# Sample value products with the probabilities standing, and the combination of three groups batched over tiles

## What is computed

```python
# latent attention of a sample token: rows = 1024 cached rows of its batch and the new one
p = mla_probs(q, k_nope, kr, inv, mask)
ctx = einsum('bhqt,btr->bqhr', p, rows[..., :KV_LORA])      # value product, 8 heads, 128 features
o_mla = einsum('bqhr,rhd->bqhd', ctx, w_uv)
# dilated attention of a sample token, for each of three groups: 128, 128 and 64 cached rows are valid
o = einsum('bhqj,bqjhe->bqhe', p, vg)                       # value product, 4 heads of 128 features
# combination of the three groups, for prompt and sample tokens
wts = softmax(stack(lses), axis=0)
o = einsum('gbsh,gbshe->bshe', wts, stack(outs))
```

## Time and profile before

| what | us |
|---|---|
| median of 3 runs (4493.37 to 4502.63) | 4498.88 |
| span of the profiled execution | 4461.3 |
| PE busy in it | 3866.2 |
| DVE busy | 2746.1 |
| ACT busy | 1193.5 |
| sample stage of latent attention | 446 to 622 |
| combination and dilated sample stage | 1411 to 1539 |

### The profile page before, as it was taken

One profiled execution on the slowest core, in us unless ns is written; L12 is line 12 of the kernel. 1 busy time (PEld: TensorE's weight loads), 2 busy tenths in 40 slices (PEclk: granted clock), 3 DMA queues, 4 the chain that ended last, 5 costly groups with the idle time before them and its releaser, 6 DMA issues.

```text
span 4461.3 us, 43547 instructions
## 1 busy us (share of the span) xinstructions
PE 3866.2 (87%) x14598; PEld 2550.7 (57%) x14598; DVE 2746.1 (62%) x6469; ACT 1193.5 (27%) x3201; POOL 861.8 (19%) x717
## 2 busy tenths in 40 slices
PE   7789879999995699977999677879999999899986
PEld 5458357798984588865444344434444445454443
DVE  1665535352345311236999997766779766976876
ACT  2356333232222101122222367621111111111111
POOL 0000000100000000001333323333333333343332
PEclk8889869997697599988999889999999999999997
DMA  4000200312114311125888879999999999999997
GB/s 152 5 2 1 55 38 22 117 45 85 60 48 152 105 43 43 62 92 194 310 316 328 326 306 354 384 418 414 413 398 379 414 412 410 373 394 414 389 357 286
DMA packets 252635, 1016.82 MB, mean 228 GB/s; under 512 B 25434, under 2 KB 100594, under 8 KB 167426
## 3 DMA queue, kind: packets, MB, share of 16 engines
q0 software_dynamic: 101520, 723.10, 40.9%
q1 hardware_dynamic: 130722, 280.49, 17.1%
q10 hardware_dynamic: 20176, 10.49, 0.8%
HBM read 964.74 MB, written 49.25 MB: 227 GB/s over the span
## 4 chain that ended last, share of the span: by engine, by line
PE 26%; DVE 15%; DMA 11%; issue 2%; ACT 2%; POOL 0%; SPq 0%; ACTq 0%; DVEq 0%
PE banks L2357 9%; PE banks L2343 8%; DMA ff_room<-in_v 8%; DVE ff_rows L2006 4%; PE banks L2332 4%; PE banks L2280 2%; DVE ff_acc L1972 2%; DMA gates_dram<-ff_room 1%; PE banks L2225 1%; DMA ff_rows<-in_uv,pk_expert 1%; DVE pk_eq L1662 1%; DVE pk_axes L1667 1%; DVE mx_x L2032 1%; PE banks L2304 1%; DVE pk_besti L1641 1%
## 5 line engine op out<-in xcount | busy, mean ns | idle before, releaser
L1904 POOL DMA_INDIRECT ff_rows<-in_uv,pk_expert x640 | 806.0, 1259 | 1507.6 <-DVE ff_acc L1972 828.4
L2006 DVE CUSTOM_DVE_ANT_0 ff_rows<-ff_rows,ff_h_row 128x1024 f32<-128x1024 f32 x648 | 766.4, 1220 | 43.9 <-DMA ff_rows<-in_uv,pk_expert 42.0
L2357 PE MATMUL banks<-ff_room,mx_x 128*128 128x512 f32 x1536 | 703.1, 609 | 59.0 <-DVE mx_x L2047 32.5
L2343 PE MATMUL banks<-mx_x,ff_room 128*128 128x384 f32 x2048 | 683.4, 487 | 10.9 <-ACT mx_x L2190 10.4
L2343 PEld LDWEIGHTS banks<-mx_x,ff_room 128*128 128x128 f32 x2048 | 389.3, 190 | 310.3 <-issue 73.5
L2332 PE MATMUL banks<-ff_rows,o_mla_tops 128*128 128x512 f32 x904 | 445.5, 642 | 138.3 <-ACT o_mla_tops L2100 134.7
L2357 PEld LDWEIGHTS banks<-ff_room,mx_x 128*128 128x128 f32 x1536 | 297.6, 195 | 420.6 <-issue 359.0
L1972 DVE SCALAR_TENSOR_TENSOR ff_acc<-ff_rows,ff_a,ff_acc 128x1024 f32<-128x1024 f32 x388 | 498.6, 1285 | 7.2
L2332 PEld LDWEIGHTS banks<-ff_rows,o_mla_tops 128*128 128x128 f32 x904 | 178.7, 206 | 355.4 <-issue 198.0
L176 PE MATMUL banks<-d_w_high,h_high 128*128 128x512 f32 (+1 forms) x648 | 275.7, 425 | 30.7 <-DVE d_w_low L183 29.8
L2088 ACT ACTIVATE ff_gelu<-ff_dots 128x2 f32<-128x2 f32 x324 | 65.7, 203 | 822.8 <-DVE ff_dots L2006 822.5
(11 more groups left out here) (379 smaller groups left out, 5942.9 us busy)
## 6 DMA issues: line engine op xcount, KB each, us to landing
ff_room<-in_uT SPq DMA_DIRECT2D x128, 512.0 KB
ff_room<-in_v SPq DMA_DIRECT2D x128, 512.0 KB
gates_dram<-ff_room SPq DMA_DIRECT2D x6, 4096.0 KB, 16.6
mx_x<-gates_dram SPq DMA_DIRECT2D x128, 192.0 KB
d_w<-in_w_dil POOLq DMA_DIRECT2D x9, 2048.0 KB, 12.7
d_w<-in_w_ada POOLq DMA_DIRECT2D x32, 512.0 KB, 4.7
ff_room<-in_w_pq SPq DMA_DIRECT2D x32, 512.0 KB
ff_rows<-in_uv,pk_expert POOLq DMA_INDIRECT x640
```

The costliest lines, as they stand in the source:

```text
L1904: pool.indirect_dma_start(out=rows[r][:, :], out_offset=None, in_=IN["uv"][:, :], in_offset=bass.IndirectOffsetOnAxis(ap=at, axis=0))\
L2006: ins = dve.tensor_tensor_reduce(rows[r][:, 0:D], rows[r][:, 0:D], h_row[i % 2][:], 1.0, 0.0, ALU.mult, ALU.add, dots[:, B % RB, j:j + 1])
L2343: ins = pe.matmul(SD[:, 0:ND], u[e % 4][:, k, :], hd[:, k, :], start=(k == 0), stop=(k == KD - 1))
L2357: ins = pe.matmul(Y[j][:, half], ad[e % 2][:, j * P:(j + 1) * P], v[e % 4][:, half_rows[half]], start=(e == 0), stop=(e == NK - 1))
```

## The change

- Latent attention: pT has 32 columns for each page and batch, 8 of them with probabilities and 24 zero (DVE zeroes the whole at the stage's start). The value product takes these 32 columns as the standing operand and the 128 columns of values as the moving one; batch 4i + k writes partitions 32k of bank i. ACT copies each bank's 128 columns to cr, and two products with picked columns of the identity turn them back and place them beside the new token's product, which now comes behind.
- Dilated sample: the same with 512 columns of values moving, for 3 groups and 8 batches; the third group holds two batches on the two halves of the partitions, and zeros in pT leave out the other one. ACT copies the first bank of results, DVE the second, and for each head two products with picked columns turn them back.
- The loads of the third group's pairs are cut in four, two for each half of the partitions.
- Combination: the statistics of all tiles are loaded once, by three DMAs of ACT's queue, in pieces of 32 bytes; the weights are made once for all tiles. The first product of each tile moves to ACT (semaphore first), in front of the copies of the values in ACT's list, and y has two buffers. ACT copies a turned tile one tile later. SP issues pairs 0 and 1 ahead of x(0), and each tile's pairs ahead of its x. DVE does a tile's keys ahead of its mixing.

```diff
+        pT = sb("pT", [P, NPAGE, NSA, M])
...
+                pe.wait_ge(s["zero"], 1)
+                for i in range(2):
+                    for j in range(NPAGE):
+                        for k in range(4):
+                            b = 4 * i + k
+                            ins = pe.matmul(c.ps[i][k * M:(k + 1) * M, 0:KVL], pT[:, j, b, :], rows[:, b * NPAGE + j, 0:KVL],
+                                            start=(j == 0), stop=(j == NPAGE - 1))
+                    ins.then_inc(s["ctx"], 1)
                 pe.matmul(c.ps[3][:, 0:R], c.lat_s[:, 0:KVL], pTn[:], start=True, stop=False)
-                for b in range(NSA):
-                    for j in range(NPAGE):
-                        last = b == NSA - 1 and j == NPAGE - 1
-                        ins = pe.matmul(c.ps[3][:, b:R:NSA], rows[:, b * NPAGE + j, 0:KVL], pT[:, j, b:R:NSA],
-                                        start=False, stop=last)
-                ins.then_inc(s["ctx"], 1)
+                of_batch = c.ps[3][:, 0:R].rearrange("p (h b) -> p h b", b=NSA)
+                picked = c.ident[:].rearrange("p (k h) -> p h k", h=M)[:, 0:MH]
+                for i in range(2):
+                    pe.wait_ge(s["ctxr"], i + 1)
+                    ins = pe.matmul(of_batch[:, :, 4 * i:4 * i + 4], cr[:, i], picked, start=False, stop=(i == 1))
+                ins.then_inc(s["ctxt"], 1)
...
+                act.wait_ge(s["zero"], 1)
+                act.activation(pT[:, :, :, 0:MH].rearrange("p j b h -> p j h b"),
+                               c.ps[4][:].rearrange("p (j h b) -> p j h b", h=MH, b=NSA), ACT.Copy).then_inc(s["ptc"], 1)
                 act.activation(pTn[:], c.ps[5][0:NSA, 0:R], ACT.Copy).then_inc(s["ptc"], 1)
+                for i in range(2):
+                    act.wait_ge(s["ctx"], i + 1)
+                    act.activation(cr[:, i], c.ps[i][:, 0:KVL], ACT.Copy).then_inc(s["ctxr"], 1)
...
+                dve.memset(pT[:], 0.0).then_inc(s["zero"], 1)
...
+        x = [sb(f"x{i}", [P, NG, GW]) for i in range(2)]
+        stats = sb("row_stats", [P, NG, NT, 2 * DH])
...
+        pT = sb("pT", [P, NG, NSA, M])
...
                 for t in range(NT):
-                    if t >= 2:
-                        sp.wait_ge(s["y"], t - 1)
-                    sp.dma_start(x[t % 2][:], c.dram["o_group"][:, t * P:(t + 1) * P, :]
-                                 .rearrange("g p w -> p g w")).then_inc(x_in[t % 2], 16)
                     for i in after[t]:
...
+                        if g < 2:
+                            sp.dma_start(kv[i % NB][:], state.rearrange("b p f -> p b f")).then_inc(kv_in[i % NB], 16)
...
+                        else:
+                            for k in range(2):
+                                at = slice(k * n, (k + 1) * n)
+                                sp.dma_start(kv[i % NB][at, 0], state[k]).then_inc(kv_in[i % NB], 16)
+                                sp.dma_start(qb[i % NB][at, 0], q[k * GW:(k + 1) * GW].unsqueeze(0).to_broadcast([n, GW]))\
+                                    .then_inc(kv_in[i % NB], 16)
+                    if t >= 2:
+                        sp.wait_ge(s["y"], t - 1)
+                    sp.dma_start(x[t % 2][:], c.dram["o_group"][:, t * P:(t + 1) * P, 0:GW]
+                                 .rearrange("g p w -> p g w")).then_inc(x_in[t % 2], 16)
...
+                def weights():
+                    nm, sm = stats[:, :, :, 0:DH], stats[:, :, :, DH:]
+                    dve.wait_ge(s["stats"], 16 * NG)
...
+                    dve.wait_ge(s["first"], t + 1)
+                    for g in range(1, NG):
                         for h in range(DH):
                             cols = slice(h * DE, (h + 1) * DE)
-                            if g == 0:
-                                ins = dve.tensor_scalar(Y[:, cols], X[:, g, cols], e[:, g, h:h + 1], None, ALU.mult)
-                            else:
-                                ins = dve.scalar_tensor_tensor(out=Y[:, cols], in0=X[:, g, cols],
-                                                               scalar=e[:, g, h:h + 1], in1=Y[:, cols],
-                                                               op0=ALU.mult, op1=ALU.add)
+                            ins = dve.scalar_tensor_tensor(out=y[t % 2][:, cols], in0=x[t % 2][:, g, cols],
+                                                           scalar=e[:, g, t, h:h + 1], in1=y[t % 2][:, cols],
+                                                           op0=ALU.mult, op1=ALU.add)
...
-                    weights(t)
+                    for n, i in enumerate(after[t]):
+                        keys(i)
+                        if t == 0 and n == 0:
+                            weights()
                     mix(t)
-                    for i in after[t]:
-                        keys(i)
...
+                dve.wait_ge(s["pv"], 2)
+                dve.tensor_copy(ors[:, 1], O[1][:]).then_inc(s["o_rows"], 1)
...
             def _(act):
-                for t in range(NT):
-                    act.wait_ge(s["diff"], t + 1)
-                    act.activation(e[:], e[:], ACT.Exp).then_inc(s["exp"], 1)
-                    for i in after[t]:
-                        g, b = pairs[i]
-                        n = KROWS[g]
-                        act.wait_ge(kv_in[i % NB], 32 * (i // NB + 1))
-                        act.activation(V[g][0:n, b:b + 2, :], kv[i % NB][0:n, :, GW:], ACT.Copy).then_inc(s["vv"], 1)
+                for g in range(NG):
+                    act.dma_start(stats[:, g], c.dram["o_group"][g, :, GW:].rearrange("(t p) w -> p t w", p=P))\
+                       .then_inc(s["stats"], 16)
+                act.dma_start(diag[:], IN["diag"][0:R]).then_inc(s["mask"], 16)
+
+                def turned(t):
                     act.wait_ge(s["turn"], t + 1)
                     act.activation(c.o_dilT[:, :, t * P:(t + 1) * P],
                                    c.ps[t % 2][:].rearrange("p (k q) -> p k q", q=P), ACT.Copy).then_inc(s["copy"], 1)
+
+                for t in range(NT):
+                    if t == 0:
+                        act.wait_ge(s["diff"], 1)
+                        act.activation(e[:], e[:], ACT.Exp).then_inc(s["exp"], 1)
+                        act.wait_ge(s["diff"], 2)
+                    act.wait_ge(x_in[t % 2], 16 * (t // 2 + 1))
+                    if t >= 2:
+                        act.wait_ge(s["turn"], t - 1)
+                    for h in range(DH):
+                        cols = slice(h * DE, (h + 1) * DE)
+                        ins = act.activation(y[t % 2][:, cols], x[t % 2][:, 0, cols], ACT.Copy, scale=e[:, 0, t, h:h + 1])
+                    ins.then_inc(s["first"], 1)
+                    for i in after[t]:
+                        act.wait_ge(kv_in[i % NB], landed(i))
+                        dst, src = values(i)
+                        act.activation(dst, src, ACT.Copy).then_inc(s["vv"], 1)
+                    if t:
+                        turned(t - 1)
+                turned(NT - 1)
...
+                act.wait_ge(s["zero"], 2)
                 act.wait_ge(s["pt"], 1)
-                act.activation(pT[:], N2[:, 0:NG * R].rearrange("p (g r) -> p g r", r=R), ACT.Copy).then_inc(s["ptc"], 1)
+                for g in range(NG):
+                    ins = act.activation(pT[:, g, :, 0:DH].rearrange("p b h -> p h b"),
+                                         N2[:, g * R:(g + 1) * R].rearrange("p (h b) -> p h b", b=NSA), ACT.Copy)
+                ins.then_inc(s["ptc"], 1)
                 act.activation(pTn[:], N3[0:NSA, 0:NG * R].rearrange("p (g r) -> p g r", r=R), ACT.Copy)\
                    .then_inc(s["ptc"], 1)
+                act.wait_ge(s["pv"], 1)
+                act.activation(ors[:, 0], O[0][:], ACT.Copy).then_inc(s["o_rows"], 1)
...
                 pe.wait_ge(s["ptc"], 2)
                 pe.wait_ge(s["vv"], len(pairs))
+                for i in range(2):
+                    for g in range(NG):
+                        for k in range(4):
+                            b = 4 * i + k
+                            ins = pe.matmul(O[i][k * M:(k + 1) * M, :], pT[:, g, b, :], V[g][:, b if g < 2 else b // 2, :],
+                                            start=(g == 0), stop=(g == NG - 1))
+                    ins.then_inc(s["pv"], 1)
+                picked = c.ident[:].rearrange("p (k h) -> p h k", h=M)
                 for h in range(DH):
                     out = N4[:, h * NSA:(h + 1) * NSA]
                     for g in range(NG):
                         pe.matmul(out, c.dvs[:, g, h * DE:(h + 1) * DE], pTn[:, g, h * NSA:(h + 1) * NSA],
                                   start=(g == 0), stop=False)
-                    for g in range(NG):
-                        n = KROWS[g]
-                        for b in range(NSA):
-                            ins = pe.matmul(out[:, b:b + 1], V[g][0:n, b, h * DE:(h + 1) * DE],
-                                            pT[0:n, g, h * NSA + b:h * NSA + b + 1],
```

(6 more changed lines are left out.)

78 lines of the change are left out of this document (42 added, 36 removed).

## The result

| | us | runs |
|---|---|---|
| before | 4473.85 (4443.77 to 4502.63) | 9 |
| after | 4434.32 (4401.72 to 4473.47) | 9 |
| ratio after/before | 0.9898, 95% 0.9863 to 0.9934 | |
| profiled execution before / after: span | 4461.3 / 4435.9 | |

What follows compares the result with a forecast made beforehand. It took PE alone at 1.2 GHz to bound the two tails, and DVE or the loads the combination loop. Latent -19.4, dilated -32.7 and loop +16 gave -36.1 us, from 4498.9 to 4462.8 us; range 4442 to 4485.

Steps and rivals of the forecast that it cites:

- The latent tail: Latent attention's value product and turning back: 7.5 + 1.2 us in place of 28.1, so -19.4 us.
- The "loss": Value products: four column streams at once fall somewhat short of 4 times, so latent 6.8 us was taken as 7.5.
- The dilated tail: Dilated attention, scores' copy to last product's end: 18.4 us against 51.1, so -32.7 us, with 8.0 for the value streams.
- the turn of the clock: Dilated value product: PE's granted clock doubles 4.1 us in, giving 7.2 us, or 8.0 with the loss.
- Rivals C: Both value products: four streams run in turn but the clock rises; sum -14.3, 4484.6 us; chance 0.12.
- rival D: Both value products: four streams run in turn and the clock stays at 1.2 GHz; sum +19.5, 4518 us; chance 0.05.
- the loop: Combination loop: values' copy waits behind the first product, which waits for x, delaying loads; +16 us, bounds +10 and +22.
- 10.2 a tile: Combination loop, third group: time per tile with 64-partition loads at 212 GB/s, against 10.7 us for the other tiles.
- Issue 0.48: Combination loop: SP's issue time counted in each tile's sum, 0.48 us of 10.7.
- My walk: Combination loop followed tile by tile: statistics at 1425, first product to 1428.8, then tiles of 10.7 and 10.2 us, L1341 at 1505.2.
- the two discounts: Combination loop: 1.2 us off for some gain in the third group, and L1341's start taken as 1503.7 instead of 1505.2.
- 37.6 more for what lies around it: Base of the total: runs' median 4498.88 us against the profiled span of 4461.3, the difference taken as untouched by the change.

Runs made afterwards that it cites:

- The run with one part: Kernel after, with the four batches' value products all written to partitions 0 to 31; latent product 16.5 us, dilated 23.1, total 4424.43 us in a single execution.
- values first: Kernel after, with ACT copying the values of a tile's pairs ahead of that tile's first product; 4428.9 us, ratio 0.9843 to before.
- loop only: Kernel before with the changed combination loop, value products of both stages left as before; 4498.39 us, ratio 1.0056 to before.

## Why the prediction was right and wrong

**Right in sign and in mechanism.** The latent tail: 6.00 us against the 7.5 forecast for the product; the turning back took 0.9 us against 1.2; the copy that spreads the probabilities over 32 columns a batch takes 1.02 us, 0.4 more than the one it replaces, and I had not counted that. From the start of that copy to the stage's last one it is 9.05 us, where it was 30.23: -21.2, against -19.4. The "loss" that I put on four streams (6.8 to 7.5) doesn't exist, and the step from 6.8 to 6.00 is the clock, which I had left at 0.50 for this product. The zeroing cost nothing: the stage as a whole won 21.3 us, the tail alone 21.2. The dilated tail: 7.66 us against 8.0, and 18.1 against 18.4 for the whole, -33.0 against -32.7. That it fits so closely is partly luck: 0.8 of the 8.0 us is the loss that isn't there. I took the turn of the clock at 4.1 us from the earlier trace rows, and the steps of after turn 4.7 us in (the rows show 0.50 to 1504.5 and 0.83 and 1.00 behind it). That four streams share the array was the step with the widest bounds (1 to 4 times), argued from sixteen loads in the earlier trace rows; its upper end held. Rivals C and D, four streams in turn, would have been 15.7 or 27.3 us for the latent product. The run with one part shows the former (16.5 us) as the price of a real series, clock and all.

**Right in mechanism, mis-sized: the loop.** Forecast +16 us (bounds +10 and +22), measured +25.2, above its upper bound. The mechanism is shown by values first: the loop falls back to the 75.9 us of before when the values' copy stands first. The sizes, tile by tile, from start to start of the first products: the first starts 16.2 us into the stage (forecast 16.4, -0.2); the step to the second is 10.9 (10.6, +0.3); the next three are 33.5 together (32.1, +1.4); the last three are 35.7 together, where I had 30.6 and took 1.2 off (+6.3); from the last first product to the scores' copy 5.5 (4.2, +1.3, of which 1.5 I had taken off the walk, from 1505.2 to 1503.7). The sum is +9. The term that was mis-sized is the tile of the third group, "10.2 a tile" less 1.2 in all, against 11.9 measured on average. Three things in it were off. "Issue 0.48" is one issue, and SP's rows show 2.4 to 2.5 us from the first of the four issues to that of x (0.9 in the other groups, with two). "0.79 MB in 3.4 us" should be 3.7 at 212 GB/s. And "the two halves now go to different partitions, which may speed that up to 2.0" gave nothing to take off: with both in one DMA the three tiles took 30.2 us instead of 35.7. My walk, without the two discounts that I gave it, came to within 6.5 us. I gave both in the same direction, and no row asked for either. (A slip that changes nothing here: in rival D the streams have to keep 49 of their 68.3 us for the change to win nothing, not over 51.)

**Wrong: the level of the number.** This, and not the loop, is why the measurement fell outside the range: the loop's error would have made the kernel slower than forecast. The failed step is "the median of the runs is 4498.88, 37.6 more for what lies around it". What lies around the span is 1.8 us: the profiled execution of after has a span of 4435.9 and a time of 4437.73. The other 36 us were the difference between executions. The three runs of before, 4493 to 4503, were all long for this kernel: nine, these three among them, gave a median of 4473.85, and nineteen others 4466.57. The profiled execution, with a span of 4461.3, was the nearer to both. No trace of the three is on record, so what made them long stays open. The traces that there are show where executions differ: up to 45 us in the untouched stage of the dilated projections, with its granted clock, 13 us in the last stage, and 24 us in the first, which lasts 78 or 102 us whatever the kernel. Busy times from 20 to 40 us, and the group of its products by one line over the first 110 us, first of before and then of values first:

```profile
20.00:40.00 20.00, 20.00 (x108) 16.60 (x108) 0.00 (x0) 4.25 (x4) 0.00 (x0) 1.00 0.66 239
```

```profile
L308 PE MATMUL banks<-silu_c,w_ada 128*128 128x9 f32 x256 | 41.4, 304 | 6.4 <-DVE silu_c L273 6.4
```

```profile
20.00:40.00 20.00, 20.00 (x66) 16.18 (x67) 0.00 (x0) 2.13 (x2) 0.00 (x0) 1.00 0.57 211
```

```profile
L308 PE MATMUL banks<-silu_c,w_ada 128*128 128x9 f32 x256 | 54.9, 358 | 6.4 <-DVE silu_c L273 6.4
```

In the same 20 us 108 matmuls are done in one and 66 in the other. Of the twelve profiled executions of this study, the one of before included, five had the long one (among them values first and loop only) and seven the short one (among them before and after). Set against the median of nine, the same sum of -36.1 would have given 4437.8, and with the loop's 25.2 us 4447. The measured 4434.3 lies below the latter by 13 us, within the 19 us by which the two ratios of after differ. So the sum was good to 7 us by stages, and the base that it was taken from was off by 25. The first bound of such a range should be the scatter of the base. The direction and the size of the change were forecast well all the same, 36 us against 29 by stages and 39.5 by medians.

## What to carry over

Small products whose outputs have few rows should be placed so that their results go to different 32-partition parts and come in turn, part after part, call by call: here four 512-column passes cost what one does. And ask what the clock does with the new calls: the exchange of operands alone, all in one part, took the latent product from 27.5 to 16.5 us, because the clock rose. When a step is moved to an engine that also frees buffers, put the freeing instruction ahead of anything that waits for a load queued behind it; one copy in the wrong place cost 25 us, and with it in the right place the step won nothing, as the loads were the bound. And take a prediction's base from the profiled execution or from many runs; three runs that agree with each other within 0.2% can all sit 25 us above the median.

## What was new about the hardware

- A small load in company: three loads of 1024 pieces of 32 bytes landed after 2.6 us alone and 12.6 us beside SP's traffic. Until SP's queue ran dry as many transfers of the one queue began as of the other (851 and 852 in 7 us).
- Two loads to the two halves of the partitions in place of one to all: 35.7 us for three tiles against 30.2. About half of that is one more issue a tile, 0.9 us each; the rest may be the rate.
- In a product of one column part the granted clock rose 4.8 us in (16.5 us for 128 passes); in the product that it replaces, with 128 columns loaded for every 8 that moved, it stayed at 0.50 for 27.4 us.
- With one column part at a time, passes of the next part begin while the part ahead has passes left; the counts fit four passes. The look-ahead's depth is inferred, not tested.
- The first stage has two durations, 78 and 102 us. In the long one its products take the time of the low clock level (L308's mean 358 ns against 304, and 66 against 108 products in 20 us) while the granted clock in the row reads 1.00 in both. What sets it is open; no run was made to find it.
- The same 3284 matmuls of the untouched dilated stage kept PE busy for 676 us at a mean granted clock of 0.93 and for 721 at 0.87, and the stage lasted 750 to 795 us in twelve executions. Only single profiled executions show this.
